# Head norms on columns, late transposes and another branch order in the mixers of a transformer on one core

## The chip, the core and the metric

The kernel runs on one core of one Trainium2 chip. The time is the device time of one execution in microseconds (us), median over runs. The core has a matrix engine (TensorE, PE in the profile, with its weight loads as PEld), VectorE (DVE), ScalarE (ACT), GpSimd (POOL) and SyncE (SP), which issues the transfers here.

## The reference

Two blocks on a sequence of 256 positions and width 1024. The first block has a recurrent mixer, cross attention and a feed-forward part. The second block has two layers, and each layer has a feed-forward part, a mixer, cross attention and a second feed-forward part. The change touches only the mixer of these two layers:

```python
y_ret = retention(...)           # 4 heads of 128: silu(g) * rms_norm_2(o), per head
y_mla = latent_attention(...)    # 8 heads of 64, softmax
y_diff = diff_attention(...)     # 4 heads of 128: rms_norm_2(o) * (1 - lambda_init), per head
branches = jnp.stack([y_ret, y_mla, y_diff], axis=2)
proj = jnp.einsum('bsnw,nwd->bsnd', branches, w_branch)
gates = jax.nn.sigmoid(gate_logits.reshape(b, s, N_BRANCH, D_MODEL))
return jnp.sum(gates * proj, axis=2) @ w_out
```

`rms_norm_2(o)` is o times 1/sqrt(mean(o^2) + 1e-6) over the 128 values of a head.

## The kernel before

Activations lie transposed: features on partitions, the 256 positions in the free dimension. Every product with weights is done in three passes of a reduced format: each fp32 operand is split into a first half and a remainder (H and L for activations, `whi` and `wlo` for weights), and high x high, low x high and high x low are summed in PSUM. The weights come as 635 units of eight tiles of 128x128. SP loads a unit into `raw` (a ring of 5), ScalarE copies its first half into `whi` (a ring of 4), VectorE subtracts to give `wlo`, and TensorE uses both. Small products of activations (scores, sums, transposes; `plain` and `transpose`) use full fp32 operands. Each of these stands in the profile as two passes.

The order of all work is one list of steps (`order`, with `mixer` for the part at hand). Each engine's program walks through this list and issues its own part of each step in that order, so an engine that waits for one step holds up all that stands behind it on the same engine. Before a step in which TensorE begins a new unit, ScalarE and VectorE split units up to four ahead (`first_halves`, `remainders`), and SP loads units up to nine ahead. `filler(n)` takes n entries of a list of weight tiles that need nothing from the steps around them; in the scores these are the 24 gate tiles (`gate2`), each a unit of 24 passes. PSUM has eight banks, taken in turn; a taker waits for the last reader of the bank.

A mixer goes as follows. It projects all inputs (names qa, rq, dq, mq, mk, mv, rv, dv, rg), with rope on VectorE. Then comes a loop of 19 steps: four retention scores, eight latent scores (`mla_score`), four differential ones (`dif_score`). For softmax heads, VectorE takes the maximum, ScalarE the exponential into `E`, VectorE scales by the reciprocal sum, TensorE transposes E (`turned2`, one step after a latent score, two after a differential one), ScalarE copies the result to `PT`, and TensorE forms the weighed sum one step later (`weighed`). For the retention heads, VectorE multiplies the scores with the decay table `DT`, which the step `load2` loads ahead of the loop. `lambda` computes the differential factor: two small VectorE instructions, one small product on TensorE, an exponential.

The head norms (`ret_norm`, `dif_norm`): ScalarE squares the head output `OR` into `SQ`; TensorE multiplies with a matrix of ones, which leaves the sum of a head in all 128 partitions (`head_sums`); ScalarE takes the root of the full 128x512 result; VectorE takes the reciprocal of each head, 128x256 (`norm_recip`); POOL (retention) or VectorE (differential) multiplies. After it `split_head` makes `BRH` on ScalarE and `BRL` on VectorE, the two halves that the branch products take. The branches run for pairs of output tiles in the order retention, latent for each pair, then the differential one for all; retention sets the sum `MG`, POOL adds the latent part, VectorE the differential one. After them come two fillers and the out rows.

## Time and profile before

| what | us |
|---|---|
| median of three runs (2095.05 to 2098.67) | 2096.44 |
| profiled execution | 2096.13 |
| its span | 2093.9 |
| TensorE busy in it | 2029.4 |
| VectorE busy in it | 1363.5 |

The span is the time from the first to the last instruction of the profile. The granted clock is the share of its full speed that TensorE was allowed; over the whole run it was 0.996. The first mixer's loop of scores starts at about 868 us, its branch tiles at 985 us; the second mixer is 761 us later. A busy TensorE counts overlapping passes, so a pass lists some 0.28 us and the next begins 0.12 us after it.

### The profile page before, as it was taken

To read this page: it belongs to the slowest core of one execution; us is meant where nothing else is said; L and a number is where in the kernel's file an instruction comes from. 1 tells how busy PE (TensorE), PEld (TensorE's weight loads), DVE (VectorE), ACT (ScalarE), POOL (GpSimd) and SP (SyncE) were. 2 spreads that over 40 slices of the span, in tenths; PEclk is the share of its full clock that TensorE was granted. 3 is DMA by queue.
4 is the path that set the end of the run, shared out by engine and by line. 5 is a ranking of instruction groups with operands and counts; after the bars stand their busy time and mean duration, and the time that the engine had idled before them with its cause. 6 is when DMAs were issued, how large, how long until landed. Compare 5 with 4: busy or idle time off the path is not lost.

```text
span 2093.9 us, 37767 instructions
## 1 busy us (share of the span) xinstructions
PE 2029.4 (97%) x15428; PEld 1894.5 (90%) x15428; DVE 1363.5 (65%) x1871; ACT 1093.0 (52%) x1702; POOL 52.3 (2%) x50
## 2 busy tenths in 40 slices
PE   7999999999999999999999999999999899998998
PEld 7989988999899889889888998999899898888997
DVE  6786866776566566767767554655477677756554
ACT  5846555554554454456456444644455455545443
POOL 0021000000000000010100000000000011000000
PEclk9999999999999999999999999999999999999999
DMA  7522454555465556434554655555555435444553
GB/s 263 171 74 82 163 186 145 203 188 187 161 221 189 186 179 203 166 111 141 181 201 145 206 184 191 199 183 183 191 183 180 157 111 169 168 166 153 182 189 121
DMA packets 98441, 359.30 MB, mean 172 GB/s; under 512 B 11160, under 2 KB 11480, under 8 KB 98008
## 3 DMA queue, kind: packets, MB, share of 16 engines
q1 hardware_dynamic: 98272, 356.90, 49.9%
q8 instruction: 124, 2.03, 0.4%
q14 instruction: 45, 0.37, 0.1%
HBM read 353.65 MB, written 1.05 MB: 169 GB/s over the span
## 4 chain that ended last, share of the span: by engine, by line
PE 79%; DVE 12%; ACT 6%; issue 2%; DMA 1%; ACTq 0%; SPq 0%; DVEq 0%
PE ps L923 15%; PE ps L924 14%; PE ps L925 14%; PE ps L988 6%; PE ps L989 6%; PE ps L990 6%; PE ps L911 5%; DVE wlo L1514 4%; PE ps L1067 2%; PE ps L1068 2%; PE ps L1074 2%; ACT whi L2223 2%; PE ps L955 1%; PE ps L956 1%; PE ps L957 1%
## 5 line engine op out<-in xcount | busy, mean ns | idle before, releaser
L1514 DVE TENSOR_TENSOR wlo<-raw,whi 128x1024 fp32r<-128x1024 f32 x635 | 771.2, 1224 | 497.8 <-ACT whi L2223 496.4
L2223 ACT ACTIVATE whi<-raw 128x1024 fp32r<-128x1024 f32 x635 | 665.1, 1056 | 385.8 <-PE ps L925 169.0
L923 PE MATMUL ps<-H,whi 128*128 128x256 f32 x2608 | 746.0, 286 | 1.7 <-DVE wlo L1514 1.7
L924 PE MATMUL ps<-L,whi 128*128 128x256 f32 x2608 | 737.7, 283 | 0.0
L925 PE MATMUL ps<-H,wlo 128*128 128x256 f32 x2608 | 737.7, 283 | 0.0
L923 PEld LDWEIGHTS ps<-H,whi 128*128 128x128 f32 x2608 | 500.0, 192 | 7.7 <-issue 4.7
L924 PEld LDWEIGHTS ps<-L,whi 128*128 128x128 f32 x2608 | 500.2, 192 | 0.5
L925 PEld LDWEIGHTS ps<-H,wlo 128*128 128x128 f32 x2608 | 500.1, 192 | 0.0
L988 PE MATMUL ps<-whi,HH 128*128 128x512 f32 x440 | 171.2, 389 | 0.0
L989 PE MATMUL ps<-whi,HL 128*128 128x512 f32 x440 | 171.2, 389 | 0.0
L990 PE MATMUL ps<-wlo,HH 128*128 128x512 f32 x440 | 171.2, 389 | 0.0
L2227 ACT ACTIVATE HH<-UP 128x512 fp32r<-128x512 f32 x55 | 34.7, 632 | 130.2 <-DVE UP L1518 130.2
L990 PEld LDWEIGHTS ps<-wlo,HH 128*128 128x128 f32 x440 | 82.6, 188 | 17.3
L988 PEld LDWEIGHTS ps<-whi,HH 128*128 128x128 f32 x440 | 82.6, 188 | 17.0
L989 PEld LDWEIGHTS ps<-whi,HL 128*128 128x128 f32 x440 | 82.6, 188 | 16.8
L1067 PE MATMUL ps<-H,whi 128*128 128x256 f32 x352 | 88.6, 288 | 3.7 <-ACT H L2227 2.7
L1068 PE MATMUL ps<-H,wlo 128*128 128x256 f32 x352 | 87.5, 285 | 0.0
L1067 PEld LDWEIGHTS ps<-H,whi 128*128 128x128 f32 x352 | 68.5, 194 | 6.4 <-issue 5.0
L1068 PEld LDWEIGHTS ps<-H,wlo 128*128 128x128 f32 x352 | 68.5, 195 | 0.0
L923 PE MATMUL ps<-mha,whi 128*128 128x256 f32 x192 | 56.0, 292 | 12.6 <-DVE wlo L1514 12.6
L923 PE MATMUL ps<-BRH,whi 128*128 128x256 f32 x192 | 56.9, 296 | 9.9 <-DVE wlo L1514 9.9
L2227 ACT ACTIVATE CV<-ps 128x512 f32<-128x512 f32 x44 | 26.4, 599 | 75.7 <-PE ps L925 69.7
(422 smaller groups left out, 2966.3 us busy)
## 6 DMA issues: line engine op xcount, KB each, us to landing
raw<-in_ws SPq DMA_DIRECT2D x635, 512.0 KB, 3.8
prow<-in_rows SPq DMA_DIRECT2D x11, 512.0 KB, 6.0
row<-in_rows SPq DMA_DIRECT2D x9, 512.0 KB, 5.3
mema<-in_memT SPq DMA_DIRECT2D x4, 512.0 KB, 5.0
mema<-in_mem2T SPq DMA_DIRECT2D x4, 512.0 KB, 7.1
memb<-in_mem2T SPq DMA_DIRECT2D x4, 512.0 KB, 5.8
DT<-in_dec SPq DMA_DIRECT2D x2, 768.0 KB, 4.9
X<-in_x SPq DMA_DIRECT2D x1, 1024.0 KB, 9.7
```

Of the source, the lines that this page charges most:

```text
L911: mm = e.matmul(o, l, r, start=start, stop=stop, skip_group_check=True)
L923: e.matmul(o, h, hs[k], start=first and k == 0, stop=False, skip_group_check=True)
L924: e.matmul(o, h, ls[k], start=False, stop=False, skip_group_check=True)
L925: mm = e.matmul(o, lo, hs[k], start=False, stop=last and end, skip_group_check=True)
L988: e.matmul(o, xh, h, start=first, stop=False, skip_group_check=True)
L989: e.matmul(o, xl, h, start=False, stop=False, skip_group_check=True)
L990: mm = e.matmul(o, xh, lo, start=False, stop=bool(names) and names[0][0] == "o", skip_group_check=True)
L1067: e.matmul(o, h, hs[k], start=k == 0 and n % 2 == 0, stop=False, skip_group_check=True)
L1068: e.matmul(o, lo, hs[k], start=False, stop=False, skip_group_check=True)
L1514: e.tensor_tensor(m.wlo[:, n % SPL, :], r, h.bitcast(F32), SUB).then_inc(*c.lo.done(n))
L2223: e.activation(m.whi[:, n % SPL, :], m.raw[:, n % RAW, :], ACT.Copy).then_inc(*c.hi.done(n))
L2227: e.activation(o, a, f, **kw).then_inc(*act.done(*names))
```

## The change

The decay table is loaded after the first head of tiles, and the first part of `lambda` is done before the dq tiles. In the loop the latent scores start two steps later (21 steps in all), and a latent transpose stands two steps behind its score, with four weight buffers (E0, EE0, E1, EE1). The sums over a head are now products of one column each, with the squares as the stationary operand: they leave the sums of 128 positions in a column of 128 partitions. ScalarE's root and VectorE's reciprocal then work on four or eight columns (`rch`). `head_rows` takes such a column, read 128 times over as stationary operand, times the identity, which leaves the inverse norms along the free dimension in all partitions; VectorE multiplies with this out of PSUM for both kinds of heads. Five of the eight tiles of the latent branch are fillers at the end of the loop; the other three, then the retention branch and the differential one follow it.

```diff
-                elif step[0] in ("keys", "values", "gate2"):
+                elif step[0] in ("keys", "values", "gate2", "branch"):
...
     o.put("hide", l)
+    o.put("load2", l)
     o.put("qa_out", l, 0)
...
     o.put("q_latent", l)
+    o.put("lambda", l, 0)
     o.work("dq", l, 0)
...
-    o.put("lambda", l, 0)
     o.filler(1)
     o.put("lambda", l, 1)
-    o.put("load2", l)
-    for step in range(19):
+    o.fill.append([[("branch", l, 1, m)] + [("branch_out", l, 1, m - 1)] * (m % 2) for m in range(8)])
+    for step in range(21):
+        if step >= 14:
+            if step < 20:
+                o.put("turned2", l, step - 8)
         if step < 4:
             o.put("ret_score", l, step)
-        elif step < 12:
-            o.put("mla_score", l, step - 4)
-        elif step < 16:
-            o.put("dif_score", l, step - 12)
+        elif 6 <= step < 14:
+            o.put("mla_score", l, step - 6)
+        elif 14 <= step < 18:
+            o.put("dif_score", l, step - 14)
         if 1 <= step < 5:
             o.put("ret_sum", l, step - 1)
-        if 5 <= step < 13:
-            o.put("turned2", l, step - 5)
-        elif 14 <= step < 18:
-            o.put("turned2", l, step - 6)
-        if 6 <= step < 14:
-            o.put("weighed", l, step - 6)
-            o.put("weighed", l, step - 7)
-        if 5 <= step < 14:
-            o.put("ret_norm", l, step - 5)
-        if step >= 17:
-            o.put("dif_norm", l, step - 17)
-        if step == 5:
+        if 8 <= step < 14:
+            o.put("turned2", l, step - 8)
+        if step >= 9:
+            o.put("weighed", l, step - 9)
+        if step in (5, 7, 8):
+            o.put("ret_norm", l, {5: 0, 7: 1, 8: 2}[step])
+        if step in (9, 11):
+            o.put("ret_split", l, step - 9)
+        if step >= 19:
+            o.put("dif_norm", l, step - 19)
+        if step == 10:
             rope("dq", 6)
         if step == 6:
             o.put("mem_load", 3 + 2 * l)
-        o.filler(2 if step > 11 else 1)
-    o.filler(10 ** 6)
+        o.filler(2 if step > 13 else 1)
     o.put("row", s)
     prepare(3 + 2 * l, value_fillers)
-    order2 = [(m, n) for m in range(0, 8, 2) for n in (0, 1)] + [(m, 2) for m in range(0, 8, 2)]
-    for at, (m, n) in enumerate(order2):
-        for q in range(2):
-            o.work("branch", l, n, m + q)
-        o.put("branch_out", l, n, m)
-        if at < 4:
+    branches = o.fill.pop(0)
+    for at, steps in enumerate(branches):
+        for step in steps:
+            (o.work if step[0] == "branch" else o.put)(*step)
+        if at < 2:
             o.put("dif_norm", l, 2 + at)
-        if at == 7:
+    for n in (0, 2):
+        for m in range(0, 8, 2):
+            for q in range(2):
+                o.work("branch", l, n, m + q)
+            o.put("branch_out", l, n, m)
+            if n == 2 and m:
+                o.put("merged", l, m - 2)
+        if n == 0:
             o.put("prow", ("c", l))
-        if n == 2 and m:
-            o.put("merged", l, m - 2)
     o.put("merged", l, 6)
     o.filler(2)
     for k in range(4):
...
+        self.rch = kept("rch", [128, 8])
...
+    def weights_of(self, n):
+        return (self.E[0], self.EE[0], self.E[1], self.EE[1])[n % 4] if n < 8 else self.E[n % 2]
...
-        E = m.E[n % 2]
+        E = m.weights_of(n)
...
-    def head_sums(l, which, j):
-        bank = bank_for("head_sums", l, which, j)
-        e.wait_ge(*act.after("head_sq", l, which, j + 1))
-        for r in range(2):
-            plain(pair(bank)[:, r, :], C["ones"], m.SQ[:, j + r, :], *[("head_sums", l, which, j)] * r)
+    def head_sums(l, which, heads):
+        bank = bank_for("head_sums", l, which, heads[0])
+        e.wait_ge(*act.after("head_sq", l, which, heads[-1]))
+        for q in heads:
+            for tb in range(2):
+                at = 2 * q + tb
+                plain(bank[:, at:at + 1], m.SQ[:, q, 128 * tb:128 * tb + 128], C["ones"][:, 0:1],
+                      *[("head_sums", l, which, heads[0])] * (q == heads[-1] and tb == 1))
+    def head_rows(l, which, j):
+        bank = bank_for("head_rows", l, which, j)
+        e.wait_ge(*dve.after("rch", l, which, 0 if which == 0 else j))
+        for q in range(2):
+            for tb in range(2):
+                at = 2 * (j + q) + tb
+                plain(pair(bank)[:, q, 128 * tb:128 * tb + 128], m.rch[:, at:at + 1].broadcast_to([128, 128]), C["ident"],
+                      *[("head_rows", l, which, j)] * (q == tb == 1))
 
     def ret_norm(l, p):
         if p == 0:
-            head_sums(l, 0, 0)
-            head_sums(l, 0, 2)
+            head_sums(l, 0, (0, 1, 2, 3))
+        else:
+            head_rows(l, 0, 2 * (p - 1))
 
     def dif_norm(l, p):
-        if p in (0, 3):
-            head_sums(l, 2, 2 * (p == 3))
+        j = 2 * (p // 2)
+        if p % 2 == 0:
+            head_sums(l, 2, (j, j + 1))
+        else:
+            head_rows(l, 2, j)
...
-        s4, E = m.s4[n % 2], m.E[n % 2]
+        s4, E = m.s4[n % 4], m.weights_of(n)
...
-    def norm_recip(l, which, q):
-        if q % 2 == 0:
-            e.wait_ge(*act.after("head_norm", l, which, q))
-        recip(m.SQ[:, q, :], m.SQ[:, q, :], ("hr", l, which, q))
+    def head_recip(l, which, j, n):
+        a = 2 * j
+        e.wait_ge(*act.after("head_norm", l, which, j))
+        recip(m.rch[:, a:a + n], m.rch[:, a:a + n], ("rch", l, which, j))
...
     def ret_norm(l, p):
-        if p in (1, 2, 5, 6):
-            norm_recip(l, 0, {1: 0, 2: 1, 5: 2, 6: 3}[p])
-        elif p in (4, 8):
-            split_head(l, 0, 2 * (p == 8))
+        if p == 0:
+            head_recip(l, 0, 0, 8)
+        else:
+            j = 2 * (p - 1)
+            o = m.OR[:, j:j + 2, :]
+            e.wait_ge(*pe.after("head_rows", l, 0, j))
+            tt(o, o, pair(banks.of("head_rows", l, 0, j)), MUL, ("hr", l, j))
+            banks.free(dve, "head_rows", l, 0, j)
+    def ret_split(l, j):
+        split_head(l, 0, j)
 
     def dif_norm(l, p):
         li = 0.8 - 0.6 * math.exp(-0.3 * l)
-        if p in (1, 4):
-            norm_recip(l, 2, 0 if p == 1 else 2)
-        elif p in (2, 5):
-            j = 0 if p == 2 else 2
-            norm_recip(l, 2, j + 1)
-            own()
-            stt(m.OR[:, j:j + 2, :], m.OR[:, j:j + 2, :], 1.0 - li, m.SQ[:, j:j + 2, :], MUL, MUL, ("dn", l, j))
+        j = 2 * (p // 2)
+        o = m.OR[:, j:j + 2, :]
+        if p % 2 == 0:
+            head_recip(l, 2, j, 4)
+        else:
+            e.wait_ge(*pe.after("head_rows", l, 2, j))
+            stt(o, o, 1.0 - li, pair(banks.of("head_rows", l, 2, j)), MUL, MUL, ("dn", l, j))
+            banks.free(dve, "head_rows", l, 2, j)
             split_head(l, 2, j)
...
-        if n == 0:
+        if n == 1:
             stt(mg, g, 1.0, pair(bank), ADD, MUL, ("mg", l, i))
...
     def mla_score(l, n):
-        if n >= 2:
-            e.wait_ge(*pe.after("turned2", l, n - 2))
-        softmax(("mla_score", l, n), m.E[n % 2], m.s4[n % 2], 96 ** -0.5)
+        if n >= 4:
+            e.wait_ge(*pe.after("turned2", l, n - 4))
+        softmax(("mla_score", l, n), m.weights_of(n), m.s4[n % 4], 96 ** -0.5)
 
     def dif_score(l, h):
         i = h % 2
-        e.wait_ge(*pe.after("turned2", l, 6 + h))
+        e.wait_ge(*pe.after("turned2", l, (5, 7, 8, 9)[h]))
...
-    def head_root(l, which, j):
+    def head_root(l, which, j, n):
+        a = 2 * j
         e.wait_ge(*pe.after("head_sums", l, which, j))
-        do(m.SQ[:, j:j + 2, :], pair(banks.of("head_sums", l, which, j)), ACT.Sqrt, ("head_norm", l, which, j), bias=m.num(0),
+        do(m.rch[:, a:a + n], banks.of("head_sums", l, which, j)[:, a:a + n], ACT.Sqrt, ("head_norm", l, which, j), bias=m.num(0),
            scale=1.0 / 128)
...
@@ -2658,21 +2695,19 @@
     def ret_norm(l, p):
         if p == 0:
             table(ACT.Sqrt)
-            head_root(l, 0, 0)
-            head_root(l, 0, 2)
+            head_root(l, 0, 0, 8)
             table(ACT.Exp)
-        elif p in (4, 8):
-            j = 2 * (p == 8)
-            split_head(l, 0, j, *pool.after("rg", l, j))
+    def ret_split(l, j):
+        split_head(l, 0, j, *pool.after("rg", l, j))
 
     def dif_norm(l, p):
+        j = 2 * (p // 2)
         if p == 0:
             table(ACT.Sqrt)
-            head_root(l, 2, 0)
-        elif p == 3:
-            head_root(l, 2, 2)
-        elif p in (2, 5):
-            j = 2 * (p == 5)
+        if p % 2 == 0:
+            head_root(l, 2, j, 4)
+        else:
             split_head(l, 2, j, *dve.after("dn", l, j))
...
     def ret_norm(l, p):
-        if p in (3, 7):
-            j = 2 * (p == 7)
+        if p:
+            j = 2 * (p - 1)
             o = m.OR[:, j:j + 2, :]
-            e.wait_ge(*dve.after("hr", l, 0, j + 1))
-            tt(o, o, m.SQ[:, j:j + 2, :], MUL)
+            e.wait_ge(*dve.after("hr", l, j))
             e.wait_ge(*act.after("silu", l, j // 2))
-            e.wait_ge(*pool.now())
             tt(o, o, m.RG[:, j:j + 2, :], MUL, ("rg", l, j))
 
     def branch_out(l, n, i):
-        if n == 1:
-            e.wait_ge(*dve.after("gt", l, 1, i))
+        if n == 0:
+            e.wait_ge(*dve.after("gt", l, 0, i))
             mg = m.MG[:, i:i + 2, :]
-            tt(mg, mg, m.GT[1][i // 2][:, :, :], ADD, ("mg", l, i))
+            tt(mg, mg, m.GT[0][i // 2][:, :, :], ADD, ("mg", l, i))
...
     def load2(l):
+        e.wait_ge(*dve.after("xn", ("m", l), 1, 1))
         e.dma_start(flat(m.DT[:, :, :]), ins["dec"]).then_inc(c.land["dec", l], 16)
```

## Rows read from the trace of the kernel before

**Rows 1.** The page, busy us (share of the span) and instructions of each engine.

```profile
PE 2029.4 (97%) x15428; PEld 1894.5 (90%) x15428; DVE 1363.5 (65%) x1871; ACT 1093.0 (52%) x1702; POOL 52.3 (2%) x50
```

**Rows 2.** Waits of TensorE, whole span: us in total, times, longest us.

```profile
PE ps L923 <- DVE wlo L1514: 24.2, 15, 11.5
...
PE ps L1434 <- DVE E L1522: 6.9, 6, 2.1
...
PE ps L911 <- DVE PR L1518: 4.0, 2, 2.1
PE ps L911 <- DVE lam L1518: 3.0, 2, 1.5
```

**Rows 3.** Waits of TensorE between 976 and 1006 us.

```profile
PE ps L923 <- DVE wlo L1514: 4.9, 4, 2.7
```

**Rows 4.** Timeline of TensorE at 1766 us: start, us, instruction, idle before it.

```profile
1766.41 0.56 PE L923 MATMUL ps<-BRH,whi 128*128 128x256 f32 x1 [2.75 <-DVE wlo L1514]
```

**Rows 5.** Table of stretches: us, busy us (instructions) by engine, granted clock, DMA.

```profile
895.00:943.00 48.00, 44.56 (x328) 39.00 (x326) 34.16 (x75) 27.66 (x75) 6.86 (x4) 1.00 0.34 111
...
976.00:1005.00 29.00, 24.17 (x192) 23.29 (x190) 22.58 (x28) 17.88 (x27) 2.58 (x2) 1.00 0.39 139
...
1005.20:1008.60 3.40, 3.40 (x16) 3.40 (x17) 3.40 (x5) 1.35 (x2) 1.22 (x1) 0.50 0.63 223
1008.60:1012.00 3.40, 3.40 (x30) 3.40 (x30) 3.40 (x4) 1.06 (x1) 1.64 (x2) 1.00 0.74 248
```

**Rows 6.** Timeline at 870 to 877 us, SP's queue and VectorE.

```profile
870.86 0.42 SPq L2822 DMA_DIRECT2D DT<-in_dec  x1
875.92 0.56 DVE L1518 TENSOR_TENSOR PR<-ps,DT 128x384 f32<-128x384 f32 x1 [5.25 <-DMA DT<-in_dec]
```

**Rows 7.** Instructions on tile SQ: duration ns min/median/max, first and last start.

```profile
L911 PEld LDWEIGHTS ps<-SQ,cst x44: 188/190/192, 795.7 to 1745.8; 128*128 128x128 f32 x44
...
L1533 DVE RECIPROCAL SQ<-SQ x16: 1739/1744/1752, 906.7 to 1760.9; 128x256 f32<-128x256 f32 x16
...
L2718 POOL TENSOR_TENSOR OR<-OR,SQ x4: 2142/2146/2149, 914.2 to 1696.4; 128x512 f32<-128x512 f32 x4
L1527 DVE SCALAR_TENSOR_TENSOR OR<-OR,SQ x4: 691/693/695, 987.6 to 1762.7; 128x512 f32<-128x512 f32 x4
```

**Rows 8.** Timelines of TensorE, ScalarE and VectorE in the branch stage.

```profile
984.76 0.47 PE L923 MATMUL ps<-BRH,whi 128*128 128x256 f32 x1
...
991.50 1.28 ACT L2227 ACT_TABLE_LOAD   x1
...
996.30 1.74 DVE L1533 RECIPROCAL SQ<-SQ 128x256 f32<-128x256 f32 x1
...
1002.13 0.63 ACT L2227 ACTIVATE BRH<-OR 128x512 fp32r<-128x512 f32 x1 [6.76 <-DVE OR L1527]
...
1003.74 1.22 DVE L1514 TENSOR_TENSOR wlo<-raw,whi 128x1024 fp32r<-128x1024 f32 x1 [0.26 <-ACT whi L2223]
```

**Rows 9.** Groups by line and form: busy us, mean ns, idle before.

```profile
L1533 DVE RECIPROCAL s<-s 128x2 f32<-128x2 f32 x32 | 5.3, 166 | 32.6 <-ACT E L2227 24.8 <-ACT EE L2227 7.8
```

**Rows 10.** Timeline of TensorE at 894 us, sums over two pairs of heads.

```profile
894.53 1.89 PE L911 MATMUL ps<-SQ,cst 128*128 128x256 f32 x8
896.07 0.47 PE L923 MATMUL ps<-H,whi 128*128 128x256 f32 x1
```

**Rows 11.** Timeline of TensorE at 800 us, products of two columns.

```profile
799.99 0.50 PE L911 MATMUL ps<-cst,SQ 128*128 128x2 f32 x4
800.35 0.36 PE L923 MATMUL ps<-H,whi 128*128 128x256 f32 x1
```

**Rows 12.** Timeline of TensorE at 206 us, rows against the identity.

```profile
205.66 1.05 PE L911 MATMUL ps<-cst,rx 128*128 128x128 f32 x8
206.64 0.27 PE L911 MATMUL ps<-AR,St 64*64 64x64 f32 x2
```

More of the change, by code:

```diff
@@ L560, in mixer @@
     o.fill.append([[("gate2", l, n)] + [("gate2_out", l, n // 2)] * (n % 2) for n in range(24)])
-    o.put("lambda", l, 0)
     o.filler(1)
     o.put("lambda", l, 1)
-    o.put("load2", l)
-    for step in range(19):
+    o.fill.append([[("branch", l, 1, m)] + [("branch_out", l, 1, m - 1)] * (m % 2) for m in range(8)])
[3 more added lines that the diff above has]
+                o.put("turned2", l, step - 8)
         if step < 4:
             o.put("ret_score", l, step)
-        elif step < 12:
-            o.put("mla_score", l, step - 4)
-        elif step < 16:
-            o.put("dif_score", l, step - 12)
+        elif 6 <= step < 14:
+            o.put("mla_score", l, step - 6)
+        elif 14 <= step < 18:
+            o.put("dif_score", l, step - 14)
         if 1 <= step < 5:
             o.put("ret_sum", l, step - 1)
-        if 5 <= step < 13:
-            o.put("turned2", l, step - 5)
-        elif 14 <= step < 18:
-            o.put("turned2", l, step - 6)
-        if 6 <= step < 14:
-            o.put("weighed", l, step - 6)
-        elif step >= 15:
-            o.put("weighed", l, step - 7)
-        if 5 <= step < 14:
-            o.put("ret_norm", l, step - 5)
-        if step >= 17:
-            o.put("dif_norm", l, step - 17)
-        if step == 5:
+        if 8 <= step < 14:
[9 more added lines that the diff above has]
+        if step == 10:
             rope("dq", 6)
@@ L2199, in vector_program @@
            "ret_score": ret_score, "ret_sum": ret_sum, "mla_score": mla_score, "dif_score": dif_score, "weighed": weighed,
-           "ret_norm": ret_norm, "dif_norm": dif_norm, "branch_out": branch_out, "merged": merged}
+           "ret_norm": ret_norm, "ret_split": ret_split, "dif_norm": dif_norm, "branch_out": branch_out, "merged": merged}
     for n, (step, *a) in enumerate(STEPS):
@@ L2701, in scalar_program @@
            "rg_out": rg_out, "lambda": lam, "mla_score": mla_score, "dif_score": dif_score, "turned2": turned2,
-           "ret_sum": ret_sum, "weighed": weighed, "ret_norm": ret_norm, "dif_norm": dif_norm, "gate2_out": gate2_out, "merged": merged}
+           "ret_sum": ret_sum, "weighed": weighed, "ret_norm": ret_norm, "ret_split": ret_split, "dif_norm": dif_norm, "gate2_out": gate2_out, "merged": merged}
     for n, (step, *a) in enumerate(STEPS):
```

## The prediction

> **What bounds the kernel now.** I read the busy table first. TensorE is busy for 97% of the span, VectorE for 65% [rows 1]. So a change is worth what it takes from TensorE: its own passes, its waits, its time at the lower clock. The list of TensorE's waits comes next. Of some 56 us of waiting in the whole span, the lines that can belong to the mixers are the ones for E, PR and lam, 13.9 us together, and a part of the 24.2 us for wlo, the remainders of the weights [rows 2]. The stretch 976 to 1006 us, where the branches of the first mixer run, holds 4.9 us of wlo waits by itself [rows 3]; the longest comes again 761 us later in the second mixer [rows 4]. The table by stretches shows the same: between 976 and 1005 TensorE is busy for 24.2 of 29 us. Right behind that longest wait the granted clock is 0.50, which is 1.2 GHz: 16 matmuls start in 3.4 us, and in the next 3.4 us, at 2.4 GHz, 30 [rows 5]. The engine had stood still for 2.75 us before the clock fell.
>
> **Waits that the change removes (each mixer).**
> 1. lam: TensorE waits 3.0 us in the two mixers for two tiny VectorE instructions that stand behind the rope work [rows 2]. The change issues them before the dq tiles, many tens of us earlier. Gone: 1.5 us. VectorE does the same two instructions as before; what is late next is PR.
> 2. PR: the load of the decay table is issued at 870.86, VectorE stands 5.25 us for it, and TensorE then 2.09 us for PR, 4.0 in two mixers [rows 2, 6]. The change issues it after the first head of tiles, some 80 us earlier. Its own wait there is for Xn, which that head has needed already, so nothing queues behind it on SP but one 768 KB transfer. Its data are used 5 us after its issue [rows 6]. The weight units behind it have a ring of five raw and four split buffers, some 12 us of passes, and that hides it; I cost the move at nothing (up to 2 us if that ring were half empty). Gone: 2.0 us.
> 3. E: a transpose now follows its own scores by one step; TensorE waits 6.9 us in two mixers [rows 2]. Two steps behind, one more gate tile lies between (24 passes, at 30 in 3.4 us [rows 5] some 2.8 us) and one more set of scores, while the longest wait is 2.1 us. It needs four buffers for weights and for the small s4, and takes EE for them, free at that time. Gone: 3.45 us, if VectorE keeps up (first rival).
> 4. Branches: VectorE runs reciprocals of 128x256, eight in each mixer, 1744 ns each, sixteen and 27.9 us in all [rows 7]. Four lie in the branch stage. There ScalarE stands 6.76 us at BRH for VectorE's normed heads, its next first halves come late behind that, the remainder that TensorE waits for starts at 1003.74 and takes 1.22 us [rows 3, 8]. The change puts in the place of each pair of reciprocals one of eight or four columns (one of two columns takes 166 ns [rows 9]), drops table loads of 1.28 us in this stage, where ScalarE now changes between tanh and square root [rows 8] (the gates are over before the new roots start), and lets the latent branch, ready long before, fill this time. VectorE loses about 3.3 us of work per pair of heads; the normed multiply (693 ns [rows 7]) stays, now reading PSUM. Gone: 4.9 us.
> 5. Clock: with the 2.75 us stop gone, no fall follows. 3.4 us at half speed cost 1.7 us [rows 5].
>
> Sum: 1.5 + 2.0 + 3.45 + 4.9 + 1.7 = 13.55 us a mixer, 27.1 in two.
>
> **What it adds to TensorE.** The sums over a head were two passes of 256 columns against ones, sixteen such passes a mixer; eight take 1.54 us (894.53 to 896.07), so 3.1 us [rows 10]. Now each of eight heads has two blocks of positions: 16 products of one column, 32 passes. The nearest row is a product with two columns, four passes in 0.36 us [rows 11]: 32 x 0.09 = 2.9. That is 0.2 less: nothing is saved on TensorE by the narrow form, since the load of the stationary tile sets it. Then each inverse column is spread over a tile and multiplied with the identity, which turns it into rows: 16 products of 128 columns, 32 passes. The same form stands at 205.66: eight passes and their exit take 0.98 us [rows 12], so four groups of eight take 3.9 us. Each group of full-precision passes also makes the first weight pass behind it longer, 0.47 us in place of 0.28 [rows 10]: four new groups, 0.8 us. Together -0.2 + 3.9 + 0.8 = 4.5 us a mixer, 9.0 in two. All of it is on the path, since TensorE is the bound. No row shows a stationary operand that is one column read 128 times; its bounds are 0.11 us a pass as in rows 12 (I take this, since the shape is the same) and 0.19, the whole load as listed in rows 7, which would add 0.07 x 32 = 2.2 us a mixer, 4.5 in two.
>
> The page "TensorE: Matmul & The Clock Gate" of the Trainium skill (Part 3, The mechanism) says that a weight load overlaps running matmuls only where the row groups differ. Here all have 128 rows, so by that rule each new pass would pay its load in full. This speaks against the change; its price is the third rival's. The trace does not agree: eight passes of 128 columns come in 0.98 us [rows 12], though one load alone is listed with 0.19 us [rows 7].
>
> **What it moves.** VectorE loses 27.9 us of reciprocals and takes over four multiplies of 128x512 that POOL did in 2.15 us each; by its own multiply of that size they are 0.69 each, 2.8 us [rows 7]. Its load falls by some 24 us. ScalarE's eight roots of 128x512 become six of four or eight columns. The new waits: VectorE's small reciprocal now stands for ScalarE's root, and the root for TensorE's sums; queued behind are the remainders, which run up to three units (8.6 us) ahead of TensorE. The row products stand for that reciprocal. Between sums and rows lie, for the retention heads, at least two gate tiles and a set of scores; for the first differential pair two branch tiles and a weighed sum (2.9 + 0.6 = 3.5 us); for the last pair one branch tile, 1.45 us. Root and reciprocal need about 0.5 us if both engines are free, an estimate from the small reciprocal of rows 9, but each may be inside a remainder of 1.22 [rows 8] or a memory piece. I take a wait of 1.0 us at the last pair (bounds: 0 and 3), 2.0 in two mixers. The latent branch sets MG first and POOL adds the retention one; four such adds, at most 2.15 us each as those of rows 7, lie beside 12 us of branch tiles: nothing.
>
> **Sum.** 27.1 - 9.0 - 2.0 = 16.1 us less. The profiled execution took 2096.13 us (span 2093.9), so 2080.0; the median of the runs is 0.3 us higher. Prediction 2080 us, 0.8% faster; alone this case spans 2075 to 2085. What a measurement here can tell from no change is about 0.2%, 4 us.
>
> **Rivals.**
> A. VectorE does not keep up in the score stage, and the wait for E turns into one for wlo. For it: between 895 and 943 VectorE is busy for 34.2 of 48 us [rows 5], and a step has about 1 us more in which it stands for ScalarE's exponentials; it then has a load of nine tenths in a shorter stage. Against: 7 us of that 34.2 are the four reciprocals. Price: 6.9 us of the gain, 2080 + 6.9 = 2087 (2085 to 2091). Chance 0.15.
> B. The other side: the round trip TensorE, ScalarE, VectorE, TensorE takes as long as it takes now. Its place is the last pair of heads. In this trace the sums of that pair end at 984.76 and their first reciprocal starts at 996.30 [rows 8], 11.5 us. No pass stood for it. Now the row products would, with 1.45 us of cover: 10.1 us a mixer, 20.2 in two, and the clock falls again: 2080 - 2.0 + 20.2 + 3.4 = 2101.6. It decides against the change once this wait passes 9 us a mixer. Against: in those 11.5 us lie a table load, ScalarE's stand for the first pair and that pair's two reciprocals of 1.74, and all of these go. Chance 0.07.
> C. Weight loads are not hidden: the 64 new passes of a mixer at 0.19 in place of 0.09 and 0.12 us, 3.2 + 2.2 = 5.4, 10.9 in two: 2091. The rule above would come to this. Chance 0.05.
> D. It does not do what it says: the waits come back one for one at the next point, because ScalarE and VectorE set the pace over the mixer. 23.7 us of waits less 9.0 of passes would then both be absorbed, 2096 (2093 to 2099). Against: over all stretches of the mixer VectorE has idle time, 13.8 of 48 us in the latent scores and 6.4 of 29 in the branches [rows 5], and it gives up 12 us of work there. Chance 0.07.
>
> **How the numbers follow.** Forecast 0.66, A 0.15, B 0.07, C 0.05, D 0.07. Faster by over 0.2% (below 2092.2): forecast, A and C, 0.86; within: D, 0.07; slower: B, 0.07. The range runs from 2074 (no return wait, a little less filling between groups, some wlo waits ahead of the mixer's scores gone too) to 2092, which takes in A, C and the dear bound of the spread column.
>
> **What would show it.** In the changed profile: no TensorE wait for lam and PR; none for E, or none over 0.5 us; at most 1 us of wlo waits between the last score and the out rows; a granted clock of 1.00 behind the branch stage in both mixers; 32 passes of ps<-SQ with one column at about 0.11 us apart and 32 of ps<-rch a mixer; VectorE busy some 24 us less in all. TensorE's busy time hardly moves, since 9 us of passes are added and long ends of passes are lost. A wait for rch above 3 us in each mixer is rival B; wlo waits between 890 and 940 us are rival A; a pass of rch above 0.15 us is rival C. It is wrong if TensorE stands as long as before in places that I have not named.

## The result and the profile after

| | before | changed |
|---|---|---|
| median of 4 runs each, same chip | 2097.5 us | 2073.2 us |
| lowest to highest | 2095.05 to 2098.67 | 2071.79 to 2073.23 |
| profiled execution; its span | 2096.13; 2093.9 | 2073.18; 2071.2 |

The ratio is 0.9885, with a 95% interval of 0.9873 to 0.9897: 1.15% faster. The forecast was 2080, with a range from 2074. So the time lies 6.8 us below the forecast and 0.8 us below the range. Of the runs of the kernel before, one beside the last three experiments took 2815 us at a granted clock of 0.655; it is in no ratio, and the others of that kernel lie between 2094.78 and 2105.04.

The busy table of the changed kernel answers to [rows 1]: 96 more passes, and still TensorE is busy for about as long in a span 22.7 us shorter.

```profile
PE 2031.1 (98%) x15524; PEld 1900.8 (92%) x15524; DVE 1343.6 (65%) x1865; ACT 1086.0 (52%) x1696; POOL 49.6 (2%) x46
```

TensorE's waits over the whole span (in total, times, longest, us), first three lines. They answer to [rows 2]: PR, lam and the long E waits are gone, and most of what is left of wlo is one wait of 11.3 us, which lies in no mixer.

```profile
PE ps L933 <- DVE wlo L1542: 13.8, 7, 11.3
PE ps L1040 <- DVE Xn L1555: 8.8, 10, 6.4
PE ps L921 <- DVE U L1546: 4.2, 6, 1.6
```

The same view between 770 and 1015 us, where the first mixer lies, is only this. Both wlo waits lie in the rope stage.

```profile
PE ps L933 <- DVE wlo L1542: 0.4, 2, 0.2
PE ps L1077 <- ACT H L2263: 0.3, 1, 0.3
```

The table by stretches (us, busy us and instructions of PE, PEld, DVE, ACT, POOL, granted clock, DMA share, GB/s): the latent scores, the end of the loop with its branches, and the 3.4 us that follow. It answers to [rows 3 and 5]. TensorE is busy for 48.00 of 48 and 29.00 of 29 us, where it was 44.56 and 24.17, and 31 matmuls start in the last 3.4 us at a granted clock of 1.00, where 16 had at 0.50.

```profile
895.00:943.00 48.00, 48.00 (x371) 43.91 (x369) 34.45 (x84) 26.83 (x77) 4.54 (x2) 1.00 0.34 123
974.00:1003.00 29.00, 29.00 (x244) 28.95 (x243) 23.94 (x34) 15.82 (x25) 7.92 (x4) 1.00 0.51 188
...
1003.00:1006.40 3.40, 3.40 (x31) 3.40 (x30) 3.01 (x4) 2.06 (x3) 0.00 (x0) 1.00 0.78 280
```

The new passes, in the timeline of TensorE (start, us). Eight one-column sums begin at 982.99 and the weights behind them at 983.80; eight row passes begin at 903.95 and the weights at 904.76. Both are 0.81 us for eight, 0.101 each, with the spread column as the stationary operand too.

```profile
903.95 1.06 PE L921 MATMUL ps<-cst,rch 128*128 128x128 f32 x8
904.76 0.36 PE L933 MATMUL ps<-H,whi 128*128 128x256 f32 x1
...
982.99 0.95 PE L921 MATMUL ps<-cst,SQ 128*128 128x1 f32 x8
983.80 0.36 PE L933 MATMUL ps<-BRH,whi 128*128 128x256 f32 x1
...
985.32 1.05 PE L921 MATMUL ps<-cst,rch 128*128 128x128 f32 x8
```

The round trip of the last pair, on ScalarE and VectorE, behind the sums that end at 983.80. The root starts at 983.98, the reciprocal at 984.71, 0.91 us behind the sums; before, that took 11.5 [rows 8]. The row passes at 985.32 above carry no wait.

```profile
983.98 0.26 ACT L2263 ACTIVATE rch<-ps,cst 128x4 f32<-128x4 f32 x1 [1.28 <-PE ps L921]
...
984.71 0.17 DVE L1561 RECIPROCAL rch<-rch 128x4 f32<-128x4 f32 x1
```

Both traces divide in the same way: a mixer runs from the start of the last transpose of Xn at its head to the start of the next transpose of Xn behind it, and each pass is counted from its start to the start of the next. So a wait counts with the pass ahead of it. A mixer took 276.52 and 276.35 us and takes 264.78 and 264.79. That is 23.3 us less in two, while the span is 22.7 us shorter; outside the mixers, the changed trace has one more fall of the clock, at 148.7 us (below). By parts, in the first mixer:

| stretches of passes | before | changed | |
|---|---|---|---|
| branch passes | 42.14 | 34.87 | -7.27 |
| latent scores, with the transposes' wait for E | 9.19 | 5.07 | -4.12 |
| retention scores, with the wait for PR behind them | 5.54 | 3.39 | -2.16 |
| other units of weights, with the wait for lam | 132.01 | 130.00 | -2.01 |
| sums against ones, 22 passes to 6 | 4.00 | 1.10 | -2.89 |
| one-column products, 4 to 36 | 0.36 | 3.69 | +3.33 |
| rows, 0 to 32 | 0 | 3.24 | +3.24 |

### The profile page after: what moved, and what is told of

It is laid out like the page before. It is cut to its first block, busy times and chain, and to the rows that moved or that the text cites. A ratio compares the mean times of both kernels' runs of the same rounds, so it can differ in the third digit from the quotient of the medians.

```text
span 2071.2 us, 37945 instructions
## 1 busy us (share of the span) xinstructions
PE 2031.1 (98%) x15524; PEld 1900.8 (92%) x15524; DVE 1343.6 (65%) x1865; ACT 1086.0 (52%) x1696; POOL 49.6 (2%) x46
## 4 chain that ended last, share of the span: by engine, by line
PE 90%; DVE 5%; ACT 3%; issue 1%; DMA 0%; DVEq 0%; SPq 0%; ACTq 0%
PE ps L933 17%; PE ps L934 17%; PE ps L935 17%; PE ps L921 8%; PE ps L998 6%; PE ps L1000 6%; PE ps L999 6%; PE ps L1077 2%; PE ps L1078 2%; PE ps L1084 2%; DVE wlo L1542 2%; PE ps L965 1%; PE ps L966 1%; PE ps L967 1%; ACT whi L2259 1%; PE ps L1040 1%
```

## The experiments

Each was timed against the kernel before on its own chip, whose median there was 2097.45, 2098.59 or 2099.67 us. The ratio to it comes with each. Only two experiments had the changed kernel beside them on the same chip, so differences between rows of this table can be off by about 2 us, which is how far that median moves. The mixers are the surer measure: the two traces of the changed kernel agree in them within 0.01 us.

| kernel | us | ratio and 95% interval | its two mixers, us |
|---|---|---|---|
| changed kernel again | 2073.6 | 0.9874 (0.9858, 0.9890) | 264.79, 264.78 |
| changed, old norms | 2092.7 | 0.9975 (0.9964, 0.9986) | 273.78, 274.42 |
| before, column norms alone | 2088.1 | 0.9950 (0.9932, 0.9968) | 272.42, 273.74 |
| before, column norms and early loads | 2077.1 | 0.9893 (0.9877, 0.9909) | 266.29, 266.30 |
| changed, one step of lag | 2074.0 | 0.9880 (0.9863, 0.9898) | 264.98, 265.00 |
| changed, old branch order | 2075.6 | 0.9889 (0.9871, 0.9906) | 265.70, 265.70 |
| changed, late loads | 2085.5 | 0.9935 (0.9919, 0.9951) | 269.06, 271.78 |
| changed, rows twice | 2081.3 | 0.9913 (0.9898, 0.9928) | 268.34, 268.38 |
| changed, norms by Ln and Exp | 2078.2 | 0.9898 (0.9881, 0.9914) | 267.15, 267.13 |
| changed, idle reciprocals | 2089.0 | 0.9952 (0.9937, 0.9967) | 272.69, 272.78 |
| meant to beat the changed one | 2076.3 | 0.9890 (0.9870, 0.9910) | 266.85, 266.58 |

### Old norms in the changed order

```diff
-                plain(bank[:, at:at + 1], m.SQ[:, q, 128 * tb:128 * tb + 128], C["ones"][:, 0:1], ...)
-        recip(m.rch[:, a:a + n], m.rch[:, a:a + n], ("rch", l, which, j))
+            plain(pair(bank)[:, r, :], C["ones"], m.SQ[:, j + r, :], *[("head_sums", l, which, j)] * r)
+        recip(m.SQ[:, q, :], m.SQ[:, q, :], ("hr", l, which, q))
```

> The changed kernel with the order of the change (late transposes, table and lambda early, latent branch first, four weight buffers), but with the full-size norms of before: sums against ones, roots of 128x512, reciprocals of 128x256, POOL's multiply. TensorE then has 3.7 us fewer passes a mixer than the changed kernel (its trace: 22 passes of sums in 4.00 us, against 6.9 for columns and rows). Theory R (the full-size reciprocals were what stopped TensorE): stops for wlo come back in the branch stage and the clock may fall again, +4 to +7 us a mixer against -3.7: 2074 to 2080 us. Theory O (the order alone gives the cover): no stop comes back, 2073.2 - 7.4 = 2066 us.

It took 2092.7, 19 us above the changed kernel and more than either theory gave. Each mixer has 48 passes fewer (64 gone, 16 sums against ones back), and is 9.0 and 9.6 us longer. The waits of TensorE from 770 to 1015 us, and the instructions behind the first of them, are these: on VectorE the reciprocal of 1.74 us and a remainder stand ahead of a maximum, ScalarE stands 3.75 us for that maximum, its copy to PT comes behind the exponential, and TensorE stands for PT.

```profile
PE ps L920 <- ACT PT L2236: 5.0, 3, 3.6
PE ps L932 <- DVE wlo L1523: 4.6, 4, 3.6
...
```

```profile
905.27 1.74 DVE L1542 RECIPROCAL SQ<-SQ 128x256 f32<-128x256 f32 x1
...
909.26 0.37 ACT L2236 ACTIVATE E<-ps,s 128x128 f32<-128x128 f32 x1 [3.75 <-DVE s L1531]
```

The clock falls behind these stops too: 6.8 us at 0.50 in the first mixer and 10.2 in the second, where the kernel before had 3.4 in each. Two of these stretches, one in each mixer:

```profile
910.90:914.30 3.40, 3.40 (x14) 2.68 (x14) 1.99 (x5) 1.86 (x5) 0.00 (x0) 0.50 0.18 29
...
1668.70:1675.50 6.80, 5.98 (x25) 5.29 (x26) 4.36 (x12) 4.92 (x14) 0.67 (x1) 0.50 0.34 131
```

So the theory that the short norms pay for their passes stands. With the 3.7 us of saved passes added, the old norms cost 12.7 and 13.3 us of stops and slow clock a mixer, about twice the 4 to 7 that it gave. The theory that the other parts are what gains, and the norms cost, has fallen. The two-step lag doesn't protect TensorE: with long reciprocals the wait for E turns into one for PT. Nor does the new order of branches: a wait for wlo of 3.6 us stands in the branch stage.

### Column norms alone, in the kernel before

The same norms put into the kernel before, and nothing else.

```diff
+        self.rch = kept("rch", [128, 8])
-        if 5 <= step < 14:
-            o.put("ret_norm", l, step - 5)
+        if step in (5, 7, 8):
+            o.put("ret_norm", l, {5: 0, 7: 1, 8: 2}[step])
+        if step in (9, 11):
+            o.put("ret_split", l, step - 9)
```

> The kernel before, with only the norms on columns (and their steps); order of transposes, table load, lambda and branches as before. It has the 3.7 us of added passes a mixer. Theory R: the branch stop (5.3 us and 1.8 at half clock) and the second and third wait for E (0.4 and 1.2) go: -8.7 + 3.7 = -5.0 a mixer, 2097.5 - 10 = 2087 us; waits for lam, PR and the first for E stay. Theory O: the norms take nothing off TensorE's waits, +7.4: 2105 us.

It took 2088.1, about as expected: 9.4 us less than the kernel before. All the waits in the branch stage are gone with the order of branches as it was, and of the E waits one is left in each mixer, though the lag is one step as before:

```profile
PE ps L914 <- DVE lam L1539: 1.5, 1, 1.5
PE ps L914 <- DVE PR L1539: 1.4, 1, 1.4
PE ps L1437 <- DVE E L1543: 1.1, 1, 1.1
...
```

The granted clock now falls behind the waits for lam and PR, where it had stood at full speed in the kernel before. Two stretches of its table:

```profile
872.90:876.10 3.20, 3.20 (x16) 3.09 (x15) 0.00 (x0) 0.00 (x0) 0.00 (x0) 0.50 0.96 378
879.70:882.90 3.20, 3.20 (x17) 3.20 (x16) 1.77 (x3) 1.36 (x2) 0.00 (x0) 0.50 0.44 164
```

In the second mixer the wait for PR is 4.1 us, for 2.0 in the kernel before, though up to there the mixer's order is the same: VectorE stands 7.24 us for the table, for 5.11. What made that transfer longer is open.

```profile
1636.43 0.56 DVE L1539 TENSOR_TENSOR PR<-ps,DT 128x384 f32<-128x384 f32 x1 [7.24 <-DMA DT<-in_dec]
```

### Column norms and early loads

To the kernel above, the first `lambda` and `load2` where the change has them.

```diff
     o.put("hide", l)
+    o.put("load2", l)
...
     o.put("q_latent", l)
+    o.put("lambda", l, 0)
...
-    o.put("lambda", l, 0)
-    o.put("load2", l)
```

> The kernel before with two parts of the change: norms on columns, and the decay table and first part of lambda early. Transposes one step behind, nineteen steps, former branch order. If the parts add: the kernel with the norms alone took 2088.1 us; less 3.0 for lam, 2.8 to 4.2 for PR and the clock's falls behind them (three in that trace, 1.7 each): 2077 to 2080 us, with the wait for E of 1.1 us a mixer left and little else. If the two-step lag or the later start of the scores is needed: above 2081.

It took 2077.1. The two moved steps are worth 11.0 us here. The first mixer is 6.1 us shorter: 2.9 of it are the two waits listed above, and the rest is about what the two falls of the clock cost, 3.4 us each at half the rate. The clock now falls in neither mixer. Only 3.5 us are left to the changed kernel (2073.6 beside it), for later scores, the lag and the order of branches together. Of the 1.5 us that a mixer is longer than the changed one, 1.4 is its one wait for E, listed with 1.1:

```profile
PE ps L1437 <- DVE E L1543: 1.1, 1, 1.1
...
```

### Late loads in the changed kernel

```diff
-    o.put("load2", l)
...
-    o.put("lambda", l, 0)
...
+    o.put("lambda", l, 0)
     o.filler(1)
     o.put("lambda", l, 1)
+    o.put("load2", l)
```

> The changed kernel with the decay table loaded and the first part of lambda done where they were before the change, right ahead of the scores. Theory R: each stop returns as it was, 1.5 for lam and 2.2 for PR by the starts of passes, +3.7 us a mixer, 2080.5 us; up to 1.8 a mixer more if the clock falls behind them (2084). Rival: with the norms off VectorE one of them is hidden, +1.5 to 2.2 a mixer: 2077 us.

It took 2085.5, 12 us above the changed kernel and a little above what was expected (2084 at most). In the first mixer the waits are 2.5 us for PR and 1.5 for lam, and it is 4.3 us longer. The second is 7.0 longer: its wait for PR is 3.7, with VectorE standing 6.88 us for the table, and behind it comes a fall of the clock (1.6 us). Its waits between 1531 and 1776 us, and its table of stretches at 872 us (no fall) and 1633 us:

```profile
PE ps L921 <- DVE PR L1546: 3.7, 1, 3.7
PE ps L921 <- DVE lam L1546: 1.5, 1, 1.5
...
```

```profile
872.00:880.00 8.00, 5.51 (x41) 5.11 (x41) 2.49 (x4) 1.53 (x3) 0.00 (x0) 1.00 0.49 188
...
1633.40:1636.60 3.20, 3.20 (x18) 3.20 (x17) 1.77 (x4) 1.36 (x2) 0.00 (x0) 0.50 0.46 164
```

### One step of lag

```diff
-        if 8 <= step < 14:
-            o.put("turned2", l, step - 8)
-        if step >= 9:
+        if 7 <= step < 14:
+            o.put("turned2", l, step - 7)
+        if 8 <= step < 16:
+            o.put("weighed", l, step - 8)
+        elif step >= 17:
             o.put("weighed", l, step - 9)
```

> The changed kernel with the latent transposes one step behind their scores in place of two. Theory R (the waits for E came from the reciprocals and the roots between): at most the first wait of 2.3 us a mixer returns, and it may not, since the root and its table loads now lie in steps without a score: 2073 to 2078 us. Theory O (one step is too short by itself): the 4.1 us a mixer return, 2081.4 us.

It took 2074.0 (2072.72 to 2075.18), beside 2071.79 to 2074.42 for the changed kernel: no difference that can be told. The mixers are 0.2 us longer, and there is no wait for E. Once VectorE has no long reciprocals and the scores start two steps later, the second step of lag has nothing to hide. The kernel with column norms and early loads has this lag too, but the earlier start, and keeps a wait for E of 1.1 us; so the later start, or what moves with it, takes that one away.

### The old order of branches

Retention and latent by pairs again, then the differential branch; none of them a filler of the loop. The sum `MG` is set by retention, as before.

```diff
-    o.fill.append([[("branch", l, 1, m)] + [("branch_out", l, 1, m - 1)] * (m % 2) for m in range(8)])
...
-        o.filler(2 if step > 13 else 1)
+        o.filler(2 if step > 15 else 1)
+    o.filler(10 ** 6)
...
+    order2 = [(m, n) for m in range(0, 8, 2) for n in (0, 1)] + [(m, 2) for m in range(0, 8, 2)]
```

> The changed kernel with the branches in the former order: no branch tiles in the loop of scores, then pairs of retention and latent tiles, POOL adding the latent part; norms on columns stay, the last gate tiles lie between first sums and first rows. Theory R: no wait for wlo above 0.5 us, 2073 to 2075 us. Theory O: the branch stop returns, +5.3 us a mixer, and the clock falls, +1.8: 2084 to 2087 us.

It took 2075.6: about 2 us more, 0.9 a mixer. Its one new wait in each mixer is this, the round trip of the norms with less in front of it; from start to start it makes half of the 0.9:

```profile
...
PE ps L917 <- DVE rch L1557: 0.3, 1, 0.3
```

The kernel with column norms and early loads has the old order too, without this wait. So these 0.9 us belong to the old order with the later scores, not to the old order alone.

### The row products twice

```diff
-        for q in range(2):
+        for again, q in ((0, 0), (0, 1), (1, 0), (1, 1)):
```

> The changed kernel with each product of an inverse column with the identity done twice, the second writing the same values over the first: 32 more passes a mixer. If every pass is on the path at the 0.10 us of its row (3.24 us for 32), +6.5 us in all: 2079.7 us. Rival (these passes fill stops, TensorE waits anyway): less than +2 us, 2075.

It took 2081.3, 8 us more. In a mixer 32 passes of rows become 64 and take 6.82 us in place of 3.24: the mixer is 3.57 longer, and these passes are all of it. So what is added on TensorE is paid in full, at 0.112 us a pass here, though a load alone is listed with 0.19:

```profile
L921 PEld LDWEIGHTS ps<-cst,rch x128: 187/190/192, 900.1 to 1744.0; 128*128 128x128 f32 x128
L921 PE MATMUL ps<-cst,rch x128: 270/275/275, 900.3 to 1744.1; 128*128 128x128 f32 x128
```

### Idle reciprocals

The changed kernel, with the eight reciprocals of 128x256 done again in each mixer on data that nobody reads.

```diff
         recip(m.rch[:, a:a + n], m.rch[:, a:a + n], ("rch", l, which, j))
+        for q in (j, j + 1):
+            recip(m.SQ[:, q, :], m.SQ[:, q, :])
...
+            if j == 0:
+                for q in (2, 3):
+                    recip(m.SQ[:, q, :], m.SQ[:, q, :])
```

> The changed kernel, and VectorE does the eight reciprocals of 128x256 of each mixer too, on the squares, for nothing: two behind the small reciprocal of the retention heads, two ahead of the first multiply, two behind each small reciprocal of the differential heads. It leaves the chain of the norms short but gives VectorE back its 14 us a mixer. If VectorE's time is what stopped TensorE: stops for wlo, E or rch of 3 to 9 us a mixer, 2079 to 2091 us. If the length of the chain from sums to branch halves stopped it (ScalarE standing for the normed heads): at most 1 us a mixer, 2073 to 2075 us.

It took 2089.0, some 15.5 us more; the mixers are 7.9 and 8.0 longer. TensorE does exactly what it did. Its waits of the first mixer come next, then two VectorE lines (the two long reciprocals of the pair of heads before, and the one for rch that TensorE stands for, which starts 2.15 us behind the last pass ahead of the rows; between the two VectorE stands still for 0.69 us only), and the clock behind that wait:

```profile
PE ps L921 <- ACT PT L2268: 3.4, 2, 2.5
PE ps L921 <- DVE rch L1561: 2.2, 1, 2.2
...
```

```profile
979.79 3.33 DVE L1561 RECIPROCAL SQ<-SQ 128x256 f32<-128x256 f32 x2
...
990.16 0.17 DVE L1561 RECIPROCAL rch<-rch 128x4 f32<-128x4 f32 x1
```

```profile
991.30:994.70 3.40, 3.40 (x18) 3.40 (x17) 3.40 (x4) 0.00 (x0) 0.00 (x0) 0.50 0.47 188
```

So VectorE's time alone, in these places, stops TensorE: 8 x 1.74 = 13.9 us of VectorE on an engine that was idle for a third of the span cost 8 us of TensorE's path. In the first mixer 1.7 us of that are the fall of the clock for 3.4 us, in the second 3.4 are one of 6.8. The wait for rch is the round trip that the second rival feared; it takes VectorE's long work to make it. The old norms cost 12.7 and 13.3 us by the same count, so about three fifths are the reciprocals; the rest lies in the full-width roots, POOL's multiply and the places of the steps, which no run parts.

### Norms by logarithm and exponential

The sums go against ones as before, and ScalarE alone makes x to the power -1/2: no reciprocal, no new passes on TensorE.

```diff
-        do(m.rch[:, a:a + n], banks.of("head_sums", l, which, j)[:, a:a + n], ACT.Sqrt, ...)
+            do(m.SQ[:, j:j + 2, :], pair(banks.of("head_sums", l, which, j)), ACT.Ln, bias=m.num(0), scale=1.0 / 128)
+            do(m.SQ[:, j:j + 2, :], m.SQ[:, j:j + 2, :], ACT.Exp, ("head_norm", l, which, j), scale=-0.5)
```

> The changed kernel in its own order, but the inverse norm comes from ScalarE alone: sums against ones as before the change (rows of a head, 128x512), then ScalarE's logarithm and its exponential of -0.5 times that, both 128x512 at about 0.67 us, and VectorE's multiply. No columns, no rows against the identity, no reciprocal. Passes: -3.7 us a mixer against the changed kernel. ScalarE gets 8 x 0.67 = 5.4 us a mixer more, less what small roots took. If ScalarE has room: 2073.2 - 7.4 = 2066 us. Rival (ScalarE's in-order work then holds up the first halves, or table loads double): +3.7 or more a mixer, 2073 to 2080 us.

It took 2078.2: 5 us worse, though 3.7 us of passes a mixer are saved. ScalarE is held by full-width work and by two table loads for each use of the pair; over the run it loads tables 50 times, the changed kernel 42. By "ScalarE: Activation LUTs" of the Trainium skill (Table sets: the hidden batching unit) the logarithm and the exponential share a set and take one load; this trace shows two, at 977.62 and 979.72 us, of 1.28 each. VectorE's remainder then stands for a first half for 6.50 us, the maximum behind it is late, and TensorE stands for PT:

```profile
897.48 1.23 DVE L1524 TENSOR_TENSOR wlo<-raw,whi 128x1024 fp32r<-128x1024 f32 x1 [6.50 <-ACT whi L2230]
```

```profile
977.62 1.28 ACT L2234 ACT_TABLE_LOAD   x1
...
979.72 1.28 ACT L2234 ACT_TABLE_LOAD   x1
```

### A version meant to beat both

One step of lag, the retention norms by logarithm and exponential (their steps lie in the loop, with more around them), the differential ones on columns, and one rope piece moved into the loop.

```diff
+        if step == 2:
+            rope("dq", 4)
...
-            head_sums(l, 0, (0, 1, 2, 3))
+            ones_rows(l, 0)
+            ones_rows(l, 2)
```

> Meant to beat both kernels. The changed kernel with one-step transposes; retention norms by ones, logarithm and exponential on ScalarE (differential ones stay on columns); the third rope of the differential heads moved from ahead of the scores into their third step. Passes: 1.9 us fewer a mixer than the changed kernel; ropes: up to 0.35 of the 0.7 us of wlo stops a mixer go. If ScalarE's 2.6 us more of work in the steps without scores are hidden: -3.8 to -4.4, 2069 us. If the wait for PT of the kernel with all norms by logarithm comes from these roots and not from the lag: +2.3 a mixer, 2074 us or more.

It took 2076.3 and beats only the kernel before. 1.8 us of passes a mixer are saved, and 3.4 and 3.1 of stops for E and EE come. The trace points to the roots as their cause, but no run takes one of the three edits away: the first half at 896.11 starts behind 1.25 + 1.28 + 1.15 us of root work, and the maxima behind its remainder are late.

```profile
892.50 1.25 ACT L2269 ACTIVATE SQ<-ps,cst 128x512 f32<-128x512 f32 x2
893.76 1.28 ACT L2269 ACT_TABLE_LOAD   x1
895.06 1.15 ACT L2269 ACTIVATE SQ<-SQ 128x512 f32<-128x512 f32 x2
896.11 1.04 ACT L2265 ACTIVATE whi<-raw 128x1024 fp32r<-128x1024 f32 x1
```

### The changed kernel again

It ran unchanged beside the version meant to beat both and the kernel with column norms and early loads, as their measure.

> The changed kernel itself, beside the next two on the same chip: 2073 us, no wait of TensorE for lam, PR, E or rch in the mixers.

2073.6, with the mixers as in its first trace to 0.01 us.

## Why the prediction was right in kind and short in size

Direction and mechanism held: TensorE was the bound, so waits and the slow stretch went and passes were added, and nothing took their place. No rival came about. For each mixer the sum was 13.55 removed, 4.5 added, 1.0 of a new wait: 8.05. Measured: 15.6 removed, 3.9 added, no new wait: 11.7. The three misses all go one way, 2.0 + 0.6 + 1.0 = 3.6 us a mixer, 7.3 in two, and 2080 less 7.3 is 2072.7. The low end of the range, 2074, allowed for the last two, which alone give 2076.8; it did not allow for waits that cost more than their listed length.

- **The removed waits (the step that failed): 11.85 forecast, 13.5 gone.** I summed the waits as listed. A listed wait begins at the modelled end of the pass before it, and passes overlap: a pass lists 0.28 us where the next starts after 0.12. The longest was priced 2.75 and stood 1005.11 - 1002.09 = 3.02 us from start to start, 0.12 of it the pass: 2.90. Over the nine stops it makes most of 1.7 us a mixer: from start to start the branches' stops were 5.57 for 4.9, E 4.12 for 3.45, PR 2.16 for 2.0, lam 1.66 for 1.5. Another 0.35 lay in the other units of weights and is not assigned.

```profile
1002.09 0.28 PE L925 MATMUL ps<-BRH,wlo 128*128 128x256 f32 x1
1005.11 0.50 PE L923 MATMUL ps<-BRH,whi 128*128 128x256 f32 x1 [2.75 <-DVE wlo L1514]
```

- **The clock: 1.7 forecast, 1.7 measured** in the branch stage. That it also depends on the waits for lam and PR I did not see: in the kernel before no fall follows them, in two of the experiments one does.
- **Added passes: 4.5 forecast, 3.7 measured** (3.33 + 3.24 - 2.89), and 0.2 about the weighed sums. One column costs 0.104 a pass, for 0.09; rows 0.101, for 0.12; the lengthened first weight passes (0.8) don't show beside that, since the exit of a group was already in the 0.98 us that I had taken for eight. The dear bound of the spread column, 0.19 a pass, is out. The line of "TensorE: Matmul & The Clock Gate" of the Trainium skill (Part 3, The mechanism) that a load overlaps only where the row groups differ would have each of these full-row loads unhidden; at 0.101 to 0.112 us from start to start against 0.19 of a listed load, the measurement decides against that here.
- **The wait at the last pair: 1.0 forecast, 0 measured.** The round trip took 0.91 us to the reciprocal's start, 1.28 of idle time lying ahead of ScalarE's root. With idle reciprocals on VectorE TensorE's wait for rch is 2.2.
- **E: right sum, wrong cause.** I gave 3.45 us to the second step of lag. One step does as well. Two thirds of the listed E wait of the first mixer, 3.4 to 1.1, goes with the short norms alone, the rest with the later start of the scores or what moves with it.
- **Branches: right sum, half the cause.** The whole stop goes with the short norms, and without them the new order does not remove it; with them the new order is worth 0.9 us a mixer, not all of it there.
- **Early loads: 3.5 forecast a mixer, 5.5 to 6 measured** in the company of the short norms (11.0 and 12 us in two; 4.3 to 7.4 by the single mixers of the traces). The surplus has two parts. In the second mixer the late table came later than in the kernel before (waits for PR of 4.1 and 3.7 us for 2.0), and in three of the four mixers the clock fell behind these waits. Why either differs from the kernel before is open.
- **VectorE: 24 us less forecast, 19.9 measured** (1363.5 to 1343.6). In the score stage it is as busy as before, 34.45 of 48 us for 34.16, and TensorE never waits there: the first rival took load for lateness.

The parts are not independent. Taken away from the changed kernel, the column norms cost 19 us; put into the kernel before, they bring 9.4. The rest without them brings 4.7 of 24.

## What to carry to other kernels

Price a wait from the start of the pass before it to the start of the pass behind it, less one pass spacing; here the listed waits gave 11.85 us for 13.5. Where the bound engine shares a chain with an engine that is a third idle, look at the longest single instruction of that engine and at what stands behind it: eight of 1.74 us cost 8 us, and replacing them was worth 3.7 us of new passes on the bound engine. Whether as much time in short instructions would cost less was not run. When two parts of a change remove stops of the same engine, test each in both kernels, since one part's worth depends on the other.

## What the runs showed of the hardware

- The granted clock falls to half speed behind stops of TensorE, but not each time. The same listed stop of 1.06 us at 147 us had a fall behind it in the changed trace and none in the kernel before (rows below: the changed one, its stretch, then the one before); waits of 1.4 to 1.5 us had one in the kernel with column norms alone and none before. Even one kernel does not repeat here: the second trace of the changed kernel has the same stop, again of 1.06 us, with a clock of 1.00 and 38 matmuls behind it (last line below), and a fall at 215 us instead. What decides it was not settled. A fall of 3.4 us costs 1.6 to 1.7, and the runs of one kernel differ by 1 to 5 us, in one round by 10. The clocks on record say where much of that comes from: the 26 runs of the kernel before in the experiments' rounds have granted clocks from 0.990 to 0.995, and 0.001 less goes with about 1.3 us more (correlation -0.8).

```profile
147.56 0.34 PE L921 MATMUL ps<-U,TM 64*64 64x64 f32 x4 [1.06 <-DVE U L1546]
...
148.70:152.10 3.40, 3.40 (x17) 3.40 (x17) 2.95 (x6) 0.85 (x3) 0.00 (x0) 0.50 0.24 60
```

```profile
147.72 0.34 PE L911 MATMUL ps<-U,TM 64*64 64x64 f32 x4 [1.06 <-DVE U L1518]
```

```profile
148.70:152.10 3.40, 3.40 (x38) 3.20 (x33) 3.27 (x7) 0.86 (x2) 0.07 (x1) 1.00 0.18 39
```

- ScalarE loaded tables twice for logarithm then exponential, 1.28 us each, so this pair of functions did not share one load.
- A root of four columns takes 0.25 us on ScalarE and a reciprocal of them 0.17 on VectorE; of 128x256 the latter takes 1.74. Turning the sums onto few columns takes nearly all of the root's and reciprocal's time off both engines, for 32 passes of 0.10 us a mixer that turn them back.
